# One change to a two-block transformer kernel: the first norm's token factor applied behind the projections, and eight modulation steps in another layer

## The reference

```python
def rmsnorm(x, g):
    y = xf * lax.rsqrt(jnp.mean(xf * xf, axis=-1, keepdims=True) + EPS)
    return (y * g.astype(jnp.float32)).astype(x.dtype)

    h = rmsnorm(x, attn_norm_g[l])
    proj = h @ w_in[l]
    fq, fk, fv, f_logit, sq, sk, sv = jnp.split(proj, splits, axis=-1)
    log_f = jax.nn.log_sigmoid((f_logit + forget_bias[l])...)
    # eight heads of forgetting attention, eight of stick-breaking attention
    x = x + o @ w_out[l]
    h = rmsnorm(x, ffn_norm_g[l])
    u = causal_dwconv(h @ w_up[l], conv_w[l], conv_b[l])
    gate, val = jnp.split(u, 2, axis=-1)
    x = x + (jax.nn.silu(gate) * val) @ w_down[l]
    # second part, per layer i: mod = silu(c) @ w_ada[i] + b_ada[i]
    # h = rms_norm(x, gain) * (1 + scale) + shift
```

## Time and profile before

| what | value |
|---|---|
| device time, median of 3 runs | 1023.8 us (1023.65 to 1024.83) |
| device time of the profiled execution | 1023.69 us |
| its span in the trace | 1022.0 us |
| mean granted clock of TensorE | 0.973 |
| PE busy | 974.9 us, 95% |
| PEld busy | 947.9 us, 93% |
| DVE busy | 719.7 us, 70% |
| ACT busy | 484.3 us, 47% |
| POOL busy | 45.3 us, 4% |
| chain that ended last | PE 77%, DVE 11%, ACT 4%, DMA 4%, issue 3% |
| DMA | 207.60 MB, mean 203 GB/s |

### The profile page before, as it was taken

One profiled execution on the slowest core, in us unless ns is written; L12 is line 12 of the kernel. 1 busy time (PEld: TensorE's weight loads), 2 busy tenths in 40 slices (PEclk: granted clock), 3 DMA queues, 4 the chain that ended last, 5 costly groups with the idle time before them and its releaser, 6 DMA issues.

```text
span 1022.0 us, 18970 instructions
## 1 busy us (share of the span) xinstructions
PE 974.9 (95%) x7553; PEld 947.9 (93%) x7553; DVE 719.7 (70%) x941; ACT 484.3 (47%) x700; POOL 45.3 (4%) x79
## 2 busy tenths in 40 slices
PE   5899987999999998999999999999999989999998
PEld 4799877999999998989899999999999989999876
DVE  5699884778788875888775677687766665555544
ACT  4245553565657343555454444433444454444531
POOL 4100000000000100000100001000000000000000
PEclk8999998999999997999989999999899999999999
DMA  9678474354554981646645678789365626555441
GB/s 317 218 232 310 169 260 151 118 172 164 191 187 175 383 297 47 237 154 222 218 154 192 220 261 280 280 329 317 101 201 167 205 88 199 167 192 178 165 165 41
DMA packets 131064, 207.60 MB, mean 203 GB/s; under 512 B 4686, under 2 KB 109504, under 8 KB 124864
## 3 DMA queue, kind: packets, MB, share of 16 engines
q1 hardware_dynamic: 122784, 156.44, 45.6%
q0 software_dynamic: 6912, 50.33, 13.9%
q10 hardware_dynamic: 1312, 0.04, 0.1%
HBM read 205.74 MB, written 1.05 MB: 202 GB/s over the span
## 4 chain that ended last, share of the span: by engine, by line
PE 77%; DVE 11%; ACT 4%; DMA 4%; issue 3%; SPq 1%; ACTq 0%; DVEq 0%; POOLq 0%
PE bank L1317 22%; PE bank L1319 22%; PE bank L1318 22%; DVE w_lo L808 3%; DMA ada_raw<-in_w_ada 2%; DVE ada_acc L823 2%; PE bank L1400 2%; PE bank L1353 2%; PE bank L1355 1%; PE bank L1358 1%; PE bank L1514 1%; ACT w_hi L483 1%; DMA v_in<-in_conv_w 1%; SPq L393 1%; DVE scr L843 1%
## 5 line engine op out<-in xcount | busy, mean ns | idle before, releaser
L808 DVE TENSOR_TENSOR w_lo<-w_raw,w_hi 128x1024 fp32r<-128x1024 f32 x294 | 355.6, 1223 | 199.2 <-ACT w_hi L483 195.2
L483 ACT ACTIVATE w_hi<-w_raw 128x1024 fp32r<-128x1024 f32 x294 | 306.5, 1054 | 308.3 <-PE bank L1319 275.0
L1317 PE MATMUL bank<-act_hi,w_hi 128*128 128x256 f32 x1440 | 411.0, 285 | 1.1 <-DVE act_lo L1136 1.1
L1318 PE MATMUL bank<-act_lo,w_hi 128*128 128x256 f32 x1440 | 408.3, 284 | 0.0
L1319 PE MATMUL bank<-act_hi,w_lo 128*128 128x256 f32 x1440 | 408.2, 283 | 0.0
L1317 PEld LDWEIGHTS bank<-act_hi,w_hi 128*128 128x128 f32 x1440 | 277.2, 193 | 1.9 <-issue 1.5
L1318 PEld LDWEIGHTS bank<-act_lo,w_hi 128*128 128x128 f32 x1440 | 277.3, 193 | 0.3 <-issue 0.2
L1319 PEld LDWEIGHTS bank<-act_hi,w_lo 128*128 128x128 f32 x1440 | 277.2, 193 | 0.0
L823 DVE SCALAR_TENSOR_TENSOR ada_acc<-ada_raw,silu_c,ada_acc 128x2048 f32<-128x2048 f32 x48 | 112.6, 2346 | 9.3 <-DMA ada_raw<-in_w_ada 9.3
L1317 PE MATMUL bank<-hid_hi,w_hi 128*128 (+1 forms) x352 | 98.2, 279 | 0.4 <-DVE w_lo L808 0.4
L1318 PE MATMUL bank<-hid_lo,w_hi 128*128 (+1 forms) x352 | 98.0, 278 | 0.0
(11 more groups left out here) (263 smaller groups left out, 1283.8 us busy)
## 6 DMA issues: line engine op xcount, KB each, us to landing
ada_raw<-in_w_ada POOLq DMA_DIRECT2D x48, 1024.0 KB, 5.4
w_raw<-in_w_gate_up SPq DMA_DIRECT2D x44, 1024.0 KB, 5.1
w_raw<-in_w_down SPq DMA_DIRECT2D x33, 1024.0 KB, 5.0
w_raw<-in_w_in SPq DMA_DIRECT2D x24, 1024.0 KB, 6.7
w_raw<-in_w_up SPq DMA_DIRECT2D x22, 1024.0 KB, 5.1
w_raw<-in_w_qkv SPq DMA_DIRECT2D x12, 1024.0 KB, 7.9
w_raw<-in_w_out SPq DMA_DIRECT2D x8, 1024.0 KB, 5.0
w_raw<-in_w_o SPq DMA_DIRECT2D x4, 1024.0 KB, 5.8
```

The source lines that it names most:

```text
L483: act.activation(unit(w_hi, u), raw_half(c, h), ACT.Copy).then_inc(hi_ready, 1)
L808: dve.tensor_tensor(unit(w_lo, u), raw_half(c, h), unit(w_hi, u).bitcast(F32), ALU.subtract).then_inc(lo_ready, 1)
L1317: pe.matmul(dst, a_hi, b_hi, start=start, stop=False, skip_group_check=True)
L1318: pe.matmul(dst, a_hi, b_lo, start=False, stop=False, skip_group_check=True)
```

## The change

**The beginning.** `x` is no longer normed before it is projected. ScalarE takes the squares of `x_in` with tokens on the partitions and sums them by its accumulator (`x_square`, one instruction per half of the tokens, each half with a semaphore of its own). `act_hi` and `act_lo` are made straight from the transposed `x` in PSUM with the gain as scale (`x_hi`, `x_lo`), before the factor is known. The factor is computed on 128 x 2 values. A matmul of ones with two diagonal matrices (`x_diag`, `token_scale`) spreads it to `x_scale`, 128 x 256, in `ada_acc[:, 2]`. `place` multiplies by it: `v` by a number per partition (`x_rms`), the others by `by_token`. The forget logits get the factor and then the bias on 128 x 8 values (`f_sum`). The copy of `x` to `res` (`x_res`) stands later on VectorE, one part before and three behind the first split of chunk 1.

**TensorE** gets eight matmuls of ones by ones ahead of the transposes. The first half chunk runs as all hi\*hi, all lo\*hi (by the order in `first_half`), then those that need `w_lo`. The turning of the small vectors stands behind half chunk (1, 1), and the copies on VectorE at (2, 0), `silu` at (3, 0). The load of the gain moves to ScalarE's queue, and the small vectors are loaded behind four chunks instead of two.

**Forget rows** move in two DMAs instead of eight.

**Modulation.** `ADA_AT1` has eight places instead of 15. Steps 8 to 15 stand in the up layer's loop, which now begins at pair 3 (`straight` is 3 instead of 1), so there is one step in each of the pairs 3 to 10. The third part of `ada_acc` is set to zero later.

The diff, cut to what is spoken of:

```diff
-ADA_AT1 = [(1, 0), (1, 1), (2, 1), (3, 1), (4, 0), (4, 1), (5, 1), (6, 1), (7, 0), (7, 1), (9, 0), (10, 1), (11, 1),
-           (12, 0), (12, 1)]
+ADA_AT1 = [(4, 0), (4, 1), (5, 1), (7, 0), (7, 1), (9, 0), (10, 1), (11, 1)]
...
+            x_square(0)
+            x_hi(0)
+            x_hi(1)
+            split_unit(0, 0)
+            x_hi(2)
+            x_hi(3)
             act.wait_ge(f_landed, 32)
             act.activation(wf_hi[:], wf_raw[:], ACT.Copy).then_inc(wf_ready, 1)
-            split_unit(0, 0)
-            norm(0, 0, late=(0, 1))
+            split_unit(0, 1)
+            x_square(1)
+            act.wait_ge(x_mean, 1)
+            act.activation(x_rms[:, 2, :], x_rms[:, 1, :], ACT.Ln, scale=-2.0).then_inc(x_ln, 1)
+            act.wait_ge(x_ln, 1)
+            act.activation(x_rms[:, 3, :], x_rms[:, 2, :], ACT.Exp, scale=-0.5).then_inc(x_exp, 1)
             split(1)
...
+            dve.tensor_copy(vec[:, 0, 0:KT], bank[SPREAD_BANK][:, 0:KT]).then_inc(g_ready, 1)
+            dve.wait_ge(g_ready, 1)
+            x_lo(0)
+            x_lo(1)
+            split_unit(0, 0)
+            x_lo(2)
+            x_lo(3)
             dve.wait_ge(wf_ready, 1)
             dve.tensor_tensor(wf_lo[:], wf_raw[:], wf_hi[:].bitcast(F32), ALU.subtract).then_inc(wf_ready, 1)
...
+            split_unit(0, 1)
+            dve.wait_ge(x_squared, 2)
+            dve.tensor_scalar(x_rms[:, 1, :], x_rms[:, 0, :], -0.5 / D, -0.5 * EPS, ALU.mult, ALU.add).then_inc(x_mean, 1)
+            x_res(0)
+            dve.wait_ge(x_exp, 1)
...
+            for t in range(2):
+                dve.tensor_scalar(x_diag[:, t * P:(t + 1) * P], ident[:], x_r[:, t:t + 1], None, ALU.mult
+                                  ).then_inc(x_diag_ready, 1)
+            split_unit(1, 0)
+            for j in range(1, 4):
+                x_res(j)
+            split_unit(1, 1)
...
                         ins = dve.scalar_tensor_tensor(pad[rows, 4 * g + half:4 * g + 4:2, :], src[rows], scale,
                                                        by_token(rows), ALU.mult, ALU.mult)
...
-                        dve.tensor_scalar(f_z, bank[2][0:8, 0:T], fbias[:], None, ALU.add).then_inc(f_z_ready, 1)
+                        dve.tensor_copy(f_z, bank[2][0:8, 0:T]).then_inc(f_z_ready, 1)
+                        dve.wait_ge(x_spread, 1)
+                        link(dve.tensor_copy(x_scale, bank[SPREAD_BANK][:, 0:T]))
...
+                    if (c, h) == (2, 0):
+                        vectors_turned()
+                    if (c, h) == (3, 0):
+                        silu()
...
-            for n in range(len(ADA_AT1), 16):
-                ada(n)
...
-            gated_layer(UP1, 0, 1, True)
+            gated_layer(UP1, 0, 3, True, 8)
...
+            for _ in range(8):
+                pe.matmul(bank[0][:, 0:P], ones[:], ones[:], start=True, stop=True)
...
                     if (c, h) == (0, 1):
+                        token_scale()
                         forget_logits()
                     if (c, h) == (1, 0):
                         forget_sums()
+                    if (c, h) == (1, 1):
+                        vector_turn()
```

221 lines of the change are left out of this document (145 added, 76 removed).

## The result

The changed kernel takes 1029.6 us, the median of 16 runs (1027.15 to 1032.87), beside 1024.2 us (1019.62 to 1027.85) for the kernel before in the same job: a ratio of 1.006, 95% interval 1.0044 to 1.0076. It is slower by 6 us. Forecast was 1022.5 with a range of 1013.5 to 1027.5. The profiled execution took 1032.03 us, its span 1030.4, mean granted clock 0.972.

The account below looks back on a forecast made before the run. TensorE is busy nearly all the time, so only what makes it wait, slow down or start late counts. 1023.69 - 10.5 (beginning) - 0.2 (attention) + 9.5 (up layer) = 1022.5 us, range 1013.5 to 1027.5.

Parts of the forecast that it names:

- The mechanism of the up layer: Up layer: with a modulation step VectorE's round is 12.63 us against TensorE's 11.52, slipping 1.11 a pair; loss 9.5 us.
- attention, a gain of 0.2: Attention: without the modulation step in front, `sb_t` could start at 144.6 instead of 144.8; 0.2 us gained, at most 2.3.
- the beginning, a gain of 10.5: Up to the first scores: they start at 36.6 instead of 45.26, 8.7 us, plus 1.85 for the clock behind them.
- The 0.95: Up layer: VectorE's idle 0.95 us per pair before `hid_lo` is ScalarE's answer to `hidden`, coming however late `hidden` is.
- the 1.10: Up layer: VectorE's idle 1.10 to 1.19 us per pair before the fourth w_lo, the only part that waits for TensorE.
- Rival (a): Up layer: VectorE's idle time, 2.2 us a pair, hides the modulation steps; 1013.0 us, chance 0.15 (half-way case 1018.3, 0.13).
- Rival (b): Up layer: short waits pull TensorE's clock down; six such gaps cost 11.1 us, giving 1033.6; chance 0.08.
- rival (c): Beginning: gives only 6 us, as the waits for `f_z` and the gate each grow; 1027.3 us, chance 0.14.
- `f_z`'s wait: Beginning: new TensorE wait of 2.9 us at 20.0, until 22.9, as `forget_logits` needs `f_z` behind VectorE's splits and copies.
- its fall behind that wait: Beginning: clock drop after the 2.9 us wait at 20.0 makes half chunk (1, 0) end 1.6 us later; taken as 0.5.
- the wait for the gate: Beginning: `forget_sums` wait for the gate until about 27.3, after half chunk (1, 0) ends at 26.2; covers 1.1 us.
- 1.85 of the term: Behind the 2.29 us wait before 45.26: 3.7 us at half speed, 1.85 us lost, which the change would remove.

## Why the prediction was wrong

Measured was 1029.6 us, forecast 1022.5. The mechanism of the up layer was right to the number. Three other terms failed: the memory layout of three small tiles, which the sum had at nothing (3.5 us of loss behind the first down layer in the profile, 4.7 to 5.8 by the times); attention, a gain of 0.2 that was a loss of 3.8; and the beginning, a gain of 10.5 that was 8.4. With the old layout and nothing else changed the time lies inside the range.

**Up layer: right.** The chain (VectorE's round 12.63, slip 1.11 a pair, 10.0 late less 0.5) gave 9.5; the profile has 9.5, with the waits at the places named, 0.73 to 0.91 a pair and 2.40 at the down layer. (They add up to 7.2, since a wait is counted from the modelled end of the matmul before it, 0.28 us behind its start. From start to start the one at 252.16 lost more: that matmul comes 1.02 us behind the one before it and the next 0.22 behind, where two pitches are 0.24, so 1.00 of the 1.07 by which the pair grew.) The 0.95 stayed and the 1.10 went, as said, and filling the 0.95 took the whole loss away. Rival (a) fell. Rival (b) fell here: the granted clock is 1.00 throughout the changed kernel's up layer. The Trainium skill's observation on short waits (TensorE: Matmul & The Clock Gate, A second HAM failure mode) is not repeated by gaps of 0.7 to 0.9 between 11.5 us of work. It was near, though: with only the modulation move, the last and longest wait, 2.39, was followed by 3.4 us at half clock.

**Beginning: mis-sized, in the direction of rival (c).** The term was 10.5, the profile has 8.4. First weights came 0.9 later than taken (11.74 against 10.8; ScalarE waited 1.54 for them to land), and mean, factor and diagonals took 2.7 us on VectorE where I had 2.0, so `f_z`'s wait ended at 24.1 instead of 22.9. The larger error was the clock: I let its fall behind that wait cost 0.5, since most of it would lie under the wait for the gate. But half chunk (1, 0) took 5.4 us at half clock (24.4 to 29.8) where I had 3.3, and the gate was ready at 28.3. At full clock (1, 0) would have ended near 27.3 (24 matmuls of 0.12, an estimate; the kernel with the step in the answer wait, at full clock there, then waits 0.96 for the gate), so the wait for the gate covered 1.0 of 2.5 and the rest stood. And 1.85 of the term were a half clock that the same kernel didn't show in its second profile. That figure was misread as well: the stretch is 45.0 to 48.4, so 3.4 us at half clock and 1.7 lost. (By the prediction's own terms its bounds should read 11.0 and 7.2, not 11.1 and 7.5; nothing hangs on it.)

**Whose gain it was: wrong step.** "it waits 2.29 for the moved rows" and "The change removes that wait" are both right, but I read the wait as the DMA's and priced the smaller number of issues. It is the modulation step ahead of the copy that made it (36.38 to 38.65). The modulation move removes it by itself, so the beginning's own worth was 4.0 us of first scores (42.44 to 38.42), not 6.8. For the sum this made no difference; for the choice of what to keep of the change it does.

**Attention: wrong.** Forecast was a gain of 0.2, the profile has a loss of 3.8, of which 3.4 are the two stretches at half clock (3.4 us each, half of it lost). I had looked at the clock behind waits that the change removes and makes, and not behind waits that stay. These stayed at about equal length and turned harmful. What differs is that everything behind the beginning came some 8 us earlier; that this is the reason isn't shown. The experiment with matmuls of ones shows that the standing of TensorE at 98 brings the half clock there; it doesn't show why the same standing at 107 brings none, nor how one would have known before.

**What no step had: the layout.** The change's part list has f_bias, f_sum and x_rms at no cost. They are 144 bytes where 4 were, shift hid_hi against the weights by 128, and bring 4.5 ns for each of some 1000 matmuls in two down layers and some 380 in two output projections, less where before was at 117.8 itself. The runs give 4.7 us (kernel before with after's layout) and 5.8 by the ratios (changed kernel with before's). Without it the changed kernel is at 1.0003, that is 1024 to 1025 us, within the range and near the forecast. With it, it lies outside. That nearness is partly luck and no proof of the other terms: the beginning and attention were off by 6.1 together in the changed kernel's profile, and the profile of this kernel lacks the half clock at 24 and at 140 that both profiles of the changed kernel have.

So by size: up layer +9.5 as forecast, beginning and attention together -4.6 instead of -10.7 in the profile, and behind the first down layer +3.5 where the sum had nothing: 1023.7 + 9.5 - 4.6 + 3.5 = 1032.1, the profiled 1032.0.

## What to carry to other kernels

Look for the cover of a moved step inside the other engine's answer time: VectorE's 0.95 us behind `hidden` was idle and could be filled, the rest of its round couldn't. When a wait is for a DMA, follow the chain back to what was queued ahead of its source before pricing the DMA. And measure the pitch of a stream of matmuls from start to start in each kernel that one compares: where it changes with the same instructions, look at the addresses of the two operands first (at one layout it also changed between executions). Trying other places for them changes no instruction. It was worth 23 to 26 us here, more than any edit of the schedule, and one of the places tried cost some 8.

## What the runs showed of the hardware

- The pitch of 128x256 matmuls on 128*128 weights in f32 and fp32r tiles, each with a weight load of its own, is 113.3, 117.8, 118.6 or 120.0 ns in long stretches at full clock, by the place of the moving operand against the weights.
- At one layout two of these values, 113.3 and 117.8, occur for the same layer in different executions of one program, and also within one layer: in the kernel before, the pitch changed at 324.3 and 709.2, each time across a break in the stream of matmuls.
- The same wait, as long as before, is or is not followed by 3.4 us at half clock. Behind the wait for `v_tok` it was in seven of seven profiles where the wait ended between 96 and 100, and in none of seven where it ended between 102 and 108. Behind the wait of 2.3 to 2.5 us that ended at 44 to 46 it was in four of five. Behind the 2.4 us for `w_lo` at the head of the down layer it was in one of five.
- Seven small matmuls in the wait for `v_tok` kept the clock up in all six profiles that had them.
